# Per decode sample, 17 steps in place of 16 between the steps of a recurrent scan

## What is computed

```
s_c = einsum(q, k_cmp) * scale            # compressed blocks
p_c = masked_softmax(s_c);  o_c = p_c @ v_cmp
imp = einsum(p_c, overlap)                # importance of each block of 64 rows
idx = top_k(where(forced, 1e9, where(future, -1e9, imp)), 8)
s_s = einsum(q, k[selected blocks]) * scale;  o_s = masked_softmax(s_s) @ v[selected]
s_w = einsum(q, k_window) * scale;            o_w = masked_softmax(s_w) @ v_window
o   = g0 * o_c + g1 * o_s + g2 * o_w
```

## Time and profile before

| what | us |
|---|---|
| median of 3 runs (4015.6 to 4016.0) | 4015.86 |
| the profiled execution, its own time | 4015.91 |
| its span, first to last instruction | 4014.0 |
| scan stage of the first layer, about | 375 to 850 |
| scan stage of the second layer, about | 2364 to 2840 |

### The profile page before, as it was taken

How to read it: one execution, slowest core, us unless ns; L and a number is a source line. 1 busy time by engine, 2 the same in 40 slices (tenths; PEclk the granted TensorE clock), 3 DMA queues, 4 the chain that set the end, 5 groups by cost and what they waited for, 6 DMA issues and landing times. The chain is left out here.

```text
span 4014.0 us, 83833 instructions
## 1 busy us (share of the span) xinstructions
PE 3834.2 (96%) x34271; PEld 3499.2 (87%) x34271; DVE 2022.3 (50%) x4755; ACT 1124.0 (28%) x2480; POOL 1702.3 (42%) x2286
## 2 busy tenths in 40 slices
PE   8998899989999999999999989999899999999997
PEld 8988788866699999999899877888666999999997
DVE  6587544457545414414456874444574454144153
ACT  3154233347721000000212532333477210000002
POOL 5633222136764434434355321222377644344343
PEclk9998999999999999999999999999899999999998
DMA  4254433220042131131332553332200411311312
GB/s 130 85 166 161 122 93 89 70 97 7 13 123 65 46 123 54 48 132 44 110 94 90 157 172 105 83 87 71 95 11 20 133 48 48 132 48 56 120 41 95
DMA packets 201776, 349.65 MB, mean 87 GB/s; under 512 B 72898, under 2 KB 135490, under 8 KB 200514
## 3 DMA queue, kind: packets, MB, share of 16 engines
q1 hardware_dynamic: 201394, 344.29, 27.6%
HBM read 253.03 MB, written 95.90 MB: 87 GB/s over the span
## 5 line engine op out<-in xcount | busy, mean ns | idle before, releaser
L2602 POOL CAST wr_hi<-wr_raw 128x256 fp32r<-128x256 f32 x584 | 264.8, 453 | 903.7 <-PE ps L2642 898.1
L2604 POOL TENSOR_TENSOR wr_lo<-wr_raw,wr_hi 128x256 fp32r<-128x256 f32 x584 | 548.5, 939 | 46.8
L2642 PE MATMUL ps<-xh,wr_hi 128*128 128x384 f32 x2064 | 453.5, 328 | 0.0
L2642 PE MATMUL ps<-xl,wr_hi 128*128 128x384 f32 x2064 | 453.2, 327 | 0.0
L2642 PE MATMUL ps<-xh,wr_lo 128*128 128x384 f32 x2064 | 453.1, 327 | 0.0
L1374 POOL TENSOR_TENSOR rc_CT<-rc_AT,rc_masks 128x256 f32<-128x256 f32 x192 | 136.4, 730 | 528.7 <-DVE rc_AT L1409 411.8
L2709 ACT ACTIVATE de_c<-de_c 128x1088 f32<-128x1088 f32 (+1 forms) x44 | 49.0, 1114 | 1098.1 <-DVE de_c L2819 1098.1
L2642 PEld LDWEIGHTS ps<-xh,wr_hi 128*128 128x128 f32 x2064 | 349.1, 188 | 0.3
L2642 PEld LDWEIGHTS ps<-xh,wr_lo 128*128 128x128 f32 x2064 | 348.9, 188 | 0.0
L2642 PEld LDWEIGHTS ps<-xl,wr_hi 128*128 128x128 f32 x2064 | 348.7, 188 | 0.0
L2642 PE MATMUL ps<-de_mixh,wr_hi 128*128 128x384 f32 (+3 forms) x1440 | 321.3, 331 | 8.1 <-DVE de_mixl L2744 8.1
(11 more groups left out here) (456 smaller groups left out, 7609.0 us busy)
## 6 DMA issues: line engine op xcount, KB each, us to landing
sa_kvp<-in_cache SPq DMA_DIRECT2D x128, 256.0 KB
scr_xres<-de_x SPq DMA_DIRECT2D x56, 544.0 KB, 2.7
de_x<-scr_xres SPq DMA_DIRECT2D x56, 544.0 KB, 3.6
wr_raw<-in_w_gate SPq DMA_DIRECT2D x42, 512.0 KB, 3.6
wr_raw<-in_w_up SPq DMA_DIRECT2D x42, 512.0 KB, 3.6
rc_arbk<-scr_arbk SPq DMA_DIRECT2D x32, 512.0 KB, 4.7
wr_raw<-in_w_down SPq DMA_DIRECT2D x32, 512.0 KB, 3.7
pr_raw<-in_w_rw SPq DMA_DIRECT2D x28, 512.0 KB, 4.4
```

The lines of the kernel that those rows point to most:

```text
L2602: pool.tensor_copy(hi[:, k, :], raw[:, k, :]).then_inc(w_hi, 1)
L2604: pool.tensor_tensor(lo[:, k, :], raw[:, k, :], f32(hi[:, k, :]), ALU.subtract).then_inc(w_ready, 1)
L2642: m = pe.matmul(ps[:, (bank + b) * BANK:(bank + b) * BANK + cols], w[rows, k, :], x[rows, k, o:o + cols], start=(k == 0 and i == 0), stop= ...
```

## The change

Behind the step of S an empty step is put on PE. DVE's step of S is cut in two ahead of its wait for the exponential: L1732 to L1738 now stand in a step of their own, and everything behind it is one step later. ACT keeps both exponentials (L1641, L1643) where they were and gets an empty step behind them. POOL and SP get one empty step late in the sample. A sample has 17 steps, and SAMPLE_STEPS is 4 + 17 * 8 + 9 = 149.

```diff
-SAMPLE_STEPS = 4 + 16 * NB + 9
+SAMPLE_STEPS = 4 + 17 * NB + 9
...
                     return
-                for n in range(6):
+                for n in range(7):
                     yield
                 sp.wait_ge(out_ready, c + 1)
...
                 m.then_inc(s_scored, 1)
                 yield
+                yield
                 pe.wait_ge(imp_ready, c + 1)
...
                 act.activation(sw[:, :], sw[:, :], ACT.Exp, bias=st[:, 5:6], scale=-1.0, accum_out=st[:, 6:7]).then_inc(w_exp, 1)
                 yield
+                yield
                 act.wait_ge(p_turned, c + 1)
...
                                          op0=ALU.add, op1=ALU.min, accum_out=st[:, 5:6]).then_inc(w_masked, 1)
+                yield
                 dve.wait_ge(c_exp, c + 1)
...
                     return
-                for n in range(7):
+                for n in range(8):
                     if n == 0:
                         sort_rows(c + 1)
```

## The result

The changed kernel takes 4037.8 us (median of 4 runs, 4034.3 to 4044.1), the kernel before beside it 4015.7: ratio 1.0053 with a 95% interval of 1.0041 to 1.0065. Run again in the first experiment it came out at 4039.8, ratio 1.0054 (1.0039 to 1.0069). So it is 22 us slower, and the forecast was 20.7. The profiled execution of the changed kernel was the longest of its four, 4044.1 us with a span of 4042.2; its rows are read term by term, and the whole by the medians.

A forecast was written before the change was run, and what follows sets the result against it. PE's queue was taken to bound the kernel (busy 96% of the span). Waits at bare scan parts summed to 8.65 us per layer, plus 1.7 for the clock: 10.35, or 20.7 for two layers, giving 4036.6 us, range 4022 to 4048.

The forecast's parts named there:

- Start and sample 1: Start: T0 ahead of u waits for POOL's sort, +1.0 us; sample 1: gv waits for ACT's copies, +0.75 us net.
- Samples 2 and 3: Bare u makes st wait for copies, +0.75 us in sample 2; with S waiting behind M, +1.3 us in sample 3.
- Sample 4: DVE's block scores fall behind the output of the scan's st, so X waits 3.2 us: +2.55 us net.
- Sample 5: DVE's scores stand ahead of p's sum, so u waits about 1.85 us: +1.4 us net.
- Sample 0: DVE's importance comes behind the transposes of z1, lengthening z to the end of I: +1.2 us.
- Samples 6 and 7: Scores fall on y turns without DVE scan work, X's waits shrink by what bare z adds: 0 and +0.3 us.
- End: M of the ninth round moves behind the last st, partly beside the last output and its DMA: -0.6 us.
- The clock: New waits in samples 4 and 5 bring one more fall of PE's granted clock per layer: +1.7 us.
- Rival 2: Faster, at I and X: shrinking waits of X and for transposes give 4002.5 us at best, 4009 with half; chance 0.04.
- Rival 1: Cover elsewhere: DVE and ACT catch up in light stretches, no added clock falls, 5 us per layer, 4026 us; chance 0.21.
- rival 4: The samples' rate absorbs the added step entirely, so nothing moves: 4016 us; chance 0.05.
- rival 3: More clock falls behind light-stretch waits of samples 0, 5 and 6, three more per layer: 4045 us; chance 0.1.

The follow-up runs named there:

- the first experiment: The changed kernel once more with no edit, against the kernel before: 4039.8 us, ratio 1.0054.
- both repairs: Against the changed kernel: DVE's importance back in the step of S, and block scores one step earlier in samples 4 and 5; 4026.3 us.
- the transposes: Against the changed kernel: 20 useless transposes in PE's queue just ahead of X of sample 4; 4032.5 us.

## Why the prediction was right, and where it was not

- *The rule.* An empty step costs the wait of the scan part that it leaves bare, and no more. It held in a bare z (0.70 us), a bare G1 (1.40) and a bare u (0.69), and the run with the empty step in the MLP shows waits of the same size (1.4, 0.7, 0.8) where it leaves G1, z and u bare.
- *Start and sample 1.* In the first layer 1.1 and 0.7 (run again) against 1.0, and 0.7 against 0.75. In the second layer the start came out at -0.8 and -0.3: over turns 14 to 17 the granted clock was 0.69 before and 0.81 in the changed kernel, which I had not costed.
- *Samples 2 and 3, S behind M.* 0.5 to 0.6 and 1.3 against 0.75 and 1.3. Right.
- *Sample 4.* The term was 2.55; in the one layer where no fall followed it is 2.4, in the others 4.7 with the fall. p and X together waited 2.73 us, and slow matmuls of X added 0.46; 3.2 of wait was forecast. That it is the place in DVE's queue is shown by the run that moved it there in these two samples alone.
- *Sample 5.* 1.35 for 1.4 and u's wait 1.89 for 1.85: the working, step by step, was right.
- *Sample 0.* The term 1.2 was mis-sized. z and y with I wait 0.69 each, but z3 waits 1.19 in place of 1.76, which I had taken to stay: net 0.54.
- *Samples 6 and 7.* 0.3 was too low, 1.3 measured: y3 and I wait 0.68 for the importance and X of sample 7 waits in z3's turn (1.46), while less of X's old waits went than I took.
- *End.* -0.6 was said. First start to last group grew by 10.4 us where the turns up to the last sample sum to 10.5; the end gave -0.1 of the -0.6, because with M behind the last st it is M that ends last (860.00, L1532).
- *The clock.* I wrote one more fall per layer, 1.7 us. In sample 4 it is there, with 2.3 us. But the kernel before's own fall in sample 0 did not come back, nor in the second layer the one in sample 1 (1.55 and 1.4 us), so of the new fall 0.8 and 0.9 us net are left in the samples. In the execution run again one layer has no fall in sample 4, and both have one in sample 5.
- *The stages between.* I had put them at nothing, and against the one trace of the kernel before they took 7.0 and 4.9 us more. That is not shown to come from the change. In the twelve traces this stretch lasts 1520.0 us in the kernel before, 1522.3 and 1526.3 in the other two with 16 steps, and 1520.3 to 1528.2 in the nine with 17. It took 8.2 us more in the run whose first scan stage had grown by 0.9 (both repairs), and 0.3 in one whose first scan stage had grown by 8.3 (the transposes). Nor does the clock just behind the scan differ much, once the stretch is moved along with the scan's end. Before, then now, PE alone:

```profile
850.50:1225.50 375.00, 351.55 (x2626) 0.97 0.22 70
```

```profile
860.70:1235.70 375.00, 352.07 (x2609) 0.96 0.21 69
```

So the total of 20.7 for 22 rests on a sum of waits that was right to half a microsecond in the first layer (errors of 0.7 down and 1.0 up that cancel), and on a clock term of the right kind, whose size is partly luck: falls that I had taken to stay went, and others came where I had none. The scan stages alone, 20 us on average in two executions, agree with it too, but with 7.3 to 11.4 us for a single stage. What made the stretch between them differ from one execution to the next stays open. Rival 2 (faster) fell with X: its wait grew. Rival 1 fell with samples 3 to 5, rival 4 with the time. Of rival 3's falls, the one in sample 5 showed in one execution of two, and the one in sample 6 in neither.

## What to carry to other kernels

Where two programs are woven turn by turn into in-order queues, cost an edit by its places: for each step, what stands ahead of it in its engine's queue and which consumer comes next. 1.6 us of VectorE work at the wrong place of its queue made most of a 22 us loss, and moving it in two of eight places took 14 back; moving it everywhere made a new wait of the same size in a third. And a step's empty place is free only where the other program's part doesn't wait on its own chain.

## What I had not expected of the hardware

A short spell of light work on TensorE was often followed by the lower granted clock for some microseconds: behind 1.5 us of idle in four stages of eight, beside the long wait of sample 4 (2.7 us in most) in nine of ten, and twice it began ahead of that wait, behind one of 0.9 us and a few light groups, with TensorE busy again. A fall cost 1.4 to 2.3 us. None followed in the three places where useless transposes kept TensorE busy through most of the wait and the clock was full before it, but in a fourth the clock had fallen before they began. That filling prevents a fall is thus likely and not shown, and it bought nothing in the kernel before.
